# Expert 0's rows turned by one-hot products, gate and up weights in runs of 4 KB, rows of x taken with a step of two

## The chip, the core and the metric

The kernel runs on one core of a Trainium2 chip. The metric is the device time of one execution in microseconds. Five engines run their own instruction streams and meet at semaphores: TensorE (PE: products, with PEld for the loads of its fixed operand), VectorE (DVE), ScalarE (ACT), GpSimd (POOL) and SyncE (SP). SP's and GpSimd's streams also issue the DMA transfers.

## What is computed

One layer of a hybrid model on 512 tokens of width 1024, in f32: norm, input projection, sliding-window attention beside chunkwise retention, output projection with a residual, norm (its result is called h2), then a mixture of 16 gated experts, a residual and a last norm. The part that matters here is the mixture:

```python
p_group = softmax(hf @ rg_w + rg_b)             # 4 groups
g_prob, g_idx = top_k(p_group, 1)
e_logits = (hf @ re_w + re_b)                   # 4 experts in each group
...
top_p, top_i = top_k(softmax(sel), 2)           # two experts of that group
w = g_prob * top_p / sum(top_p)
...
for e in range(16):
    y = (silu(h @ w_gate[e]) * (h @ w_up[e])) @ w_down[e]
    out = out + combine[:, e:e + 1] * y
```

The kernel computes each expert only for the tokens that chose it.

## The kernel before, in words

**Products in two parts.** An f32 operand is split into a high part (a rounded copy, made by ScalarE) and a low part (the rest, made by VectorE), and a product is three products: high by high, high by low, low by high (`triple`, lines 1493 to 1497). So each weight passes through ScalarE (`split`, line 890) and VectorE (`split`, line 1302) before TensorE can use it.

**The dense part** (0 to 235 us) works through 15 groups of weights, `STEPS`; the last tiles of the output projection (`N1 - 2`, `N1 - 1`) interleave with the router's logits (line 1664), the second norm (`norm2`, line 1173) and the gate (`gate`, line 1198).

**The expert part.** An expert's weights are six chunks of 1 MB: two of gate, two of up, two of down. They are numbered n = 0, 1, ... in the order in which TensorE uses them: gate of expert 0 is 0 and 1, up 2 and 3, gate of expert 1 is 4 and 5, down of expert 0 is 6 and 7, and so on, six further for each expert. SP loads them into a ring of twelve raw slots (lines 461 to 486), ScalarE and VectorE split them into rings of three high and three low slots. A chunk is 12 products of 512 columns. So the split of chunk n waits for product n - 3.

The order within a step of expert e is written out by hand for each engine, with c = 0 to 5 for the chunks 6e + 4 + c:
- TensorE (`step`, line 1817): up product, transposes of `hid` and of the rows for expert e + 2 (`turn_rows`, line 1786), the gate product of e + 1 around them, the down product.
- ScalarE (`step`, line 902): six splits, the high part of the turned rows (`rows_hi`) and of the turned hidden tile, `silu`; and at the end the two halves of `y` (line 929), which scale the result by the token's weight in `row_info` and so wait for `info_ready`.
- VectorE (`step`, line 1382): six splits, `hid` = silu times up, the low parts of the hidden tile (`row_lo`) and of the rows (`rows_lo`).
- GpSimd (`traffic`, line 616): gathers the rows for expert e + 4 (`gather`), then copies `row_info` (`info_ready`), then scatters `y`. `gather` and `send_rows` read an expert's length, in quarters of 128, from field 3 of `meta` (`by_length`, line 580).

**Between the two parts.** For each token VectorE finds its two experts (`gate`: `pair_hot`, `pair_any`) and its place in their lists (`find_ranks`, from products with a triangle of ones), then marks that place in a one-hot tile (`mark`, line 1237). TensorE multiplies these with token numbers (`list_fields`) and gets, for each expert, the list of its tokens; VectorE copies it to `meta` (line 1322, `lists_ready`). h2 itself has gone to DRAM by then (line 564), and GpSimd gathers from it the rows of experts 0 and 1 (line 575). TensorE turns them (line 1856 on), ScalarE and VectorE split them, and the first product starts. `keep_clock` (line 1505) issues 33 products whose result nobody reads. While the gather runs, VectorE computes the weights of the tokens (lines 1325 to 1350). After the first rows and split 2 it makes the slots for long lists (1357 to 1364) and the flags `over`, which tell whether a list is longer than 128 (1366 to 1379, `over_set`); ScalarE waits for `over_set` before its first `silu` (line 935), since `route`, which these instructions use, lies in the buffer of `y`. SP holds its loads from chunk 8 on until the rows of expert 0 have landed (line 470).

**Names in the diff.** `h2_buf`: two buffers for h2, used in turn, that become `x_rows`, the gathered rows. `route`: VectorE's working area. `y_buf`: the two buffers for `y`.

Of the kernel before, what the change touches and what calls it, by code (L numbers as in the profile page):

```python
# [134 lines left out]
def build(nc, x, norm1_g, w_in, attn_sinks, rel_bias, ret_gn_g, w_out, norm2_g, rg_w, rg_b, re_w, re_b,  # L135
          w_gate, w_up, w_down, final_g, table, out):
    ctx = ExitStack()
    with ctx:
# [11 lines left out]
        def dram(name, shape, dt):  # L150
# [23 lines left out]
        y_buf = [nc.alloc_sbuf_tensor_at("y0", [P, D], F32, offset=at_hi + 2560 * 4),  # L174
                 nc.alloc_sbuf_tensor_at("y1", [P, D], F32, offset=at_lo + 2560 * 4)]
# [42 lines left out]
        h2_buf = [region(O_XG, D), region(O_XG + D, D)]  # L218
# [3 lines left out]
        x_rows = h2_buf  # L222
# [27 lines left out]
        route = y_buf[0][:, 0:1024]  # L250
# [21 lines left out]
        w_gate_v = w_gate.rearrange("a e (k p) n -> (a e) p k n", p=P)  # L272
        w_up_v = w_up.rearrange("a e (k p) n -> (a e) p k n", p=P)
# [28 lines left out]
        h2_out = [h2_out, sem("h2_out1")]  # L302
# [4 lines left out]
        hot_ready, index_ready = sem("hot_ready"), sem("index_ready")  # L307
        weights_set, weights_made, info_made = (sem(n) for n in ("weights_set", "weights_made", "info_made"))
# [88 lines left out]
        def _(sp):  # L397
# [48 lines left out]
            def load_expert(kind, e, half, slot):  # L446
                w = {"g": w_gate_v, "u": w_up_v}
                if kind == "d":
                    sp.dma_start(as_chunks(raw(slot), 2 * SEG), w_down_v[e][:, 2 * half:2 * half + 2, :]).then_inc(w2_in[slot], 16)
                else:  # L450
                    sp.dma_start(as_chunks(raw(slot)), w[kind][e][:, 4 * half:4 * half + 4, :]).then_inc(w2_in[slot], 16)
# [9 lines left out]
            for n in range(RING2):  # L461
# [8 lines left out]
                if n == RING2 - 4:  # L470
                    sp.wait_ge(rows_in[0], 16)
# [16 lines left out]
            def load_unit(r, e, c):  # L488
                for half in range(2):
                    for i, w in enumerate((w_gate_v, w_up_v)):  # L490
                        sp.dma_start(as_chunks(raw(2 * i + half)), w[bass.ds(e, 1), :, 4 * half:4 * half + 4, :]
                                     .rearrange("e p k n -> (e p) k n")).then_inc(ov_w, 16)
# [19 lines left out]
        def _(pool):  # L512
# [49 lines left out]
            for t in range(T - 1):  # L562
                pool.wait_ge(h2_ready, t + 1)
                pool.dma_start(h2_dram[t * P:(t + 1) * P, :], h2_buf[t % 2]).then_inc(h2_out[t % 2], 16)
            index_records(1, 0, EARLY)
            pool.wait_ge(h2_ready, T)
            pool.dma_start(h2_dram[(T - 1) * P:, :], h2_buf[(T - 1) % 2]).then_inc(h2_out[(T - 1) % 2], 16)
            index_records(2, EARLY, T)

            last_token, last_row = pool.to_reg(S - 1), pool.to_reg(2 * S - 1)  # L570
            for b in range(2):
                pool.wait_ge(h2_out[b], 16 * T // 2)
            pool.wait_ge(lists_ready, 1)
            for b in range(2):
                pool.indirect_dma_start(x_rows[b], None, h2_dram, bass.IndirectOffsetOnAxis(ap=meta[:, 4 * b:4 * b + 1], axis=0),
                                        bounds_check=last_token, oob_is_err=False).then_inc(rows_in[b], 16)
            pool.dma_start(gain2, bass.AP(final_g.tensor, 0, [[0, P], [1, D]])).then_inc(gain_in, 16)
            pool.wait_ge(info_made, 1)
# [16 lines left out]
            def gather(b, e):  # L595

                nc.gpsimd.tensor_copy(gather_idx[:, b:b + 1], meta[:, bass.ds(e * 4, 1)]).then_inc(idx_ready, 1)
                pool.wait_ge(idx_ready, e - 1)
# [17 lines left out]
            def traffic(b, e, gather_next, reuse, last=False):  # L616
                if gather_next:
                    pool.wait_ge(x_turned, e * 2 + 6)
                    pool.wait_ge(rows_in[b], e * 8 + (32 - 8 * b))
# [14 lines left out]
            gather(1, 3)  # L634
            for e in range(2):
# [51 lines left out]
        def _(act):  # L687
# [197 lines left out]
            act.wait_ge(gate_d, 1)  # L885
            nc.scalar.activation(route[:, 848:868], route[:, 848:868], ACT.Exp).then_inc(gate_e, 1)
            nc.scalar.activation(stat[:, 47:48], eps[:, 0:1], ACT.Silu)

# [7 lines left out]
            def rows_hi(b, wait):  # L896
                for a in range(2):
# [4 lines left out]
            def step(b, e, q, first=False, last_two=False):  # L902
# [30 lines left out]
            rows_hi(0, 1)  # L933
            split(3, 3, 16)
            act.wait_ge(over_set, 1)
# [12 lines left out]
            for i in range(2):  # L948
                act.wait_ge(info_ready, E - 1 + i)
                if i:  # L950
                    act.wait_ge(y_sent[0], 16 * (E // 2 - 1))
# [33 lines left out]
        def _(dve):  # L985
# [187 lines left out]
            def norm2(t):  # L1173
# [3 lines left out]
                if t >= 2:  # L1177
                    dve.wait_ge(h2_out[t % 2], 16)
                nc.vector.scalar_tensor_tensor(h2_buf[t % 2], res_t[:, t, :], rms[:, T + t:T + t + 1], gain2,
# [18 lines left out]
            def gate(t0, t1):  # L1198
# [23 lines left out]
                nc.vector.tensor_scalar(pair_any[:, t0 * E:t1 * E], flat, 2.0, None, ALU.is_lt).then_inc(pair_ready, 1)  # L1222
                pairs = [P, 2, (t1 - t0) * E]
# [4 lines left out]
            def find_ranks(t0, t1, ahead):  # L1228
# [6 lines left out]
                step_done(nc.vector.tensor_reduce(rank_tiles[:, :, t0:t1], picked_tiles[:, :, t0:t1, :], AX_X, ALU.add))  # L1235

# [72 lines left out]
            def rows_lo(b, wait):  # L1309
                for a in range(2):  # L1310
                    row_lo(xt[b][1][:, 4 * a:4 * a + 4, :], 4 + a, xt[b][0][:, 4 * a:4 * a + 4, :], x_hi, wait + a, x_lo)

            find_ranks(0, EARLY, ps[:, 1, 0:EARLY * E])
            mark(0)
            norm2(T - 1)
            gate(EARLY, T)
            mark(1)
            find_ranks(EARLY, T, ps[:, 2, 0:(T - EARLY) * E])
            for t in range(EARLY, T):
                mark(t)  # L1320
            dve.wait_ge(lists_made, 1)
# [3 lines left out]
            step_done(nc.vector.tensor_reduce(g_top, lg[:, :, 0, :], AX_X, ALU.max))  # L1325
            nc.vector.tensor_tensor(g_exp, lg[:, :, 0, :], g_top.unsqueeze(2).to_broadcast([P, T, 4]), ALU.subtract)
# [653 lines left out]
```

## Time and profile before

| what | value |
|---|---|
| median of 3 runs (lowest, highest) | 552.3 us (551.95, 555.5) |
| profiled execution: own time, span | 552.4 us, 550.6 us |
| PE, DVE, ACT, POOL busy in the span | 98%, 77%, 64%, 17% |
| chain that ended last, by engine | PE 88%, DVE 5%, ACT 2%, DMA 2%, issue 1% |
| last tile of the output projection added to the residual (VectorE) | 235.45 |
| lists copied to `meta` (`lists_ready`) | 242.95 to 243.14 |
| first gather issued | 244.03 |
| rows of expert 0 turned from | 248.97 |
| product 0, product 4, product 5 start | 251.04, 264.24, 268.27 |
| SP issues chunk 8 | 248.95 |

Times in the lower half are microseconds from the start of the span. A matmul is shown from its start to its modelled end, and the next starts before that end, so the length of a chunk is read from start to start. "Idle" on an engine counts only where the engine is what the end waits for.

### The profile page before, as it was taken

What the parts mean: (1) busy time and instruction counts of PE and PEld (TensorE: products, weight loads), DVE (VectorE), ACT (ScalarE), POOL (GpSimd) and SP (SyncE); (2) the same over time, 40 slices, a digit from 0 to 9 for tenths busy, and PEclk for the clock granted to TensorE, in tenths of its full rate; (3) what the DMA queues carried; (4) which work ended last, traced back from release to release, by engine and by line L of the source; (5) the groups of instructions that cost most, each with busy time, mean ns of one, the idle gap of its engine ahead of it and who ended that gap; (6) DMA issues with size and microseconds to landing.
All of it is one profiled execution on the core that took longest, in us unless ns stands there. A gap on an engine that the chain in (4) does not pass through costs nothing.

```text
span 550.6 us, 7873 instructions
## 1 busy us (share of the span) xinstructions
PE 536.9 (98%) x2662; PEld 438.5 (80%) x2663; DVE 421.3 (77%) x580; ACT 353.3 (64%) x470; POOL 91.3 (17%) x113
## 2 busy tenths in 40 slices
PE   7999999999999999999999999999999999999995
PEld 5988777777877888877788888888888888888883
DVE  5654599554864753588989898988989898988986
ACT  5563654780326253355778978788778978788745
POOL 3260000000000000031412222022212222110420
PEclk9999999999999999999999999999999999999998
DMA  8999122323020237639999999999999999999796
GB/s 322 371 283 401 42 71 77 76 79 77 0 77 0 78 114 251 234 138 313 349 380 373 379 394 382 367 371 376 392 352 374 375 390 373 376 390 393 251 208 212
DMA packets 63821, 144.03 MB, mean 262 GB/s; under 512 B 3833, under 2 KB 13361, under 8 KB 63665
## 3 DMA queue, kind: packets, MB, share of 16 engines
q1 hardware_dynamic: 56528, 120.24, 61.4%
q0 software_dynamic: 7120, 22.90, 13.7%
q10 hardware_dynamic: 144, 0.52, 0.3%
q8 instruction: 15, 0.25, 0.2%
q14 instruction: 14, 0.11, 0.1%
HBM read 132.77 MB, written 14.30 MB: 267 GB/s over the span
## 4 chain that ended last, share of the span: by engine, by line
PE 88%; DVE 5%; ACT 2%; DMA 2%; issue 1%; POOL 0%; DVEq 0%; POOLq 0%
PE ps L1495 25%; PE ps L1497 24%; PE ps L1496 24%; PE ps L1502 7%; PE ps L1646 2%; PE ps L1632 2%; PE ps L1608 1%; PE ps L1578 1%; PE ps L1673 1%; DMA arena<-h_dram,meta 1%; DMA arena<-norm_g 1%; DVE lo_ring L1305 1%; DVE act_lo L1015 1%; PE ps L1896 1%; DVE res L1474 0%
## 5 line engine op out<-in xcount | busy, mean ns | idle before, releaser
L1305 DVE TENSOR_TENSOR lo_ring<-arena,hi_ring 128x2048 fp32r<-128x2048 f32 x94 | 213.8, 2288 | 26.9 <-ACT hi_ring L894 26.8
L1495 PE MATMUL ps<-hi_ring,act_hi 128*128 128x512 f32 x576 | 229.8, 399 | 1.5 <-DVE lo_ring L1305 1.1
L1497 PE MATMUL ps<-hi_ring,act_lo 128*128 128x512 f32 x576 | 224.9, 390 | 0.0
L1496 PE MATMUL ps<-lo_ring,act_hi 128*128 128x512 f32 x576 | 224.4, 390 | 0.0
L894 ACT ACTIVATE hi_ring<-arena 128x2048 fp32r<-128x2048 f32 x94 | 180.2, 1917 | 28.1 <-PE ps L1497 28.1
L1495 PEld LDWEIGHTS ps<-hi_ring,act_hi 128*128 128x128 f32 x576 | 108.3, 188 | 23.5 <-issue 2.4
L1497 PEld LDWEIGHTS ps<-hi_ring,act_lo 128*128 128x128 f32 x576 | 108.1, 188 | 23.3
L1496 PEld LDWEIGHTS ps<-lo_ring,act_hi 128*128 128x128 f32 x576 | 108.4, 188 | 20.9
L1005 DVE SCALAR_TENSOR_TENSOR lo_ring<-arena,over,hi_ring 128x512 fp32r<-128x512 f32 x40 | 29.2, 747 | 29.4 <-ACT hi_ring L708 29.2
L1015 DVE TENSOR_TENSOR act_lo<-ps,act_hi 128x512 fp32r<-128x512 f32 x56 | 36.7, 683 | 7.6 <-ACT act_hi L742 5.6
L600 POOL DMA_INDIRECT arena<-h_dram,gather_idx x14 | 34.7, 2478 | 24.0 <-issue 24.0
L1502 PE MATMUL ps<-keep,arena 128*128 128x128 f32 x268 | 36.9, 279 | 1.6 <-DMA arena<-h_dram,meta 1.2
L1502 PEld LDWEIGHTS ps<-keep,arena 128*128 128x128 f32 x268 | 30.7, 143 | 6.6 <-issue 1.9
L606 POOL DMA_INDIRECT y_dram<-y,row_info x14 | 13.2, 943 | 98.5 <-issue 98.5
L708 ACT ACTIVATE hi_ring<-arena,over 128x512 fp32r<-128x512 f32 x40 | 27.5, 718 | 0.4 <-DVE over L1035 0.4
L554 POOL DMA_DIRECT2D arena<-norm_g x1 | 0.6, 556 | 153.4 <-PE ps L1502 153.4
L1495 PE MATMUL ps<-act_hi,hi_ring 128*128 128x256 f32 (+1 forms) x64 | 22.0, 343 | 0.5 <-DVE act_lo L1015 0.5
L914 ACT ACTIVATE act_hi<-ps 128x512 fp32r<-128x512 f32 x15 | 9.0, 599 | 19.8 <-PE ps L1502 19.8
L1496 PE MATMUL ps<-act_lo,hi_ring 128*128 128x256 f32 (+1 forms) x64 | 21.5, 336 | 0.0
L1497 PE MATMUL ps<-act_hi,lo_ring 128*128 128x256 f32 (+1 forms) x64 | 21.5, 336 | 0.0
L929 ACT ACTIVATE y<-ps,row_info 128x512 f32<-128x512 f32 x28 | 19.0, 680 | 3.1 <-PE ps L1497 3.1
L1294 DVE TENSOR_TENSOR res<-res,ps 128x512 f32<-128x512 f32 x8 | 5.5, 687 | 18.6 <-PE ps L1497 18.6
(237 smaller groups left out, 523.0 us busy)
## 6 DMA issues: line engine op xcount, KB each, us to landing
arena<-w_gate SPq DMA_DIRECT2D x32, 1024.0 KB, 16.6
arena<-w_up SPq DMA_DIRECT2D x32, 1024.0 KB, 17.6
arena<-w_down SPq DMA_DIRECT2D x32, 1024.0 KB, 15.2
arena<-w_in SPq DMA_DIRECT2D x16, 512.0 KB, 7.2
y_dram<-arena POOLq DMA_DIRECT2D x8, 512.0 KB, 11.2
res<-y_dram POOLq DMA_DIRECT2D x8, 512.0 KB, 9.8
arena<-w_in SPq DMA_DIRECT2D x2, 1024.0 KB, 10.9
arena<-w_out SPq DMA_DIRECT2D x4, 512.0 KB, 6.5
```

The costliest lines, as they stand in the source:

```text
L600: by_length(e, lambda n: pool.indirect_dma_start(x_rows[b][0:n, :], None, h2_dram, bass.IndirectOffsetOnAxis(ap=gather_idx[0:n, b:b + 1], ...
L606: by_length(e, lambda n: pool.indirect_dma_start(y_dram, bass.IndirectOffsetOnAxis(ap=row_info[0:n, 4 * b + 1:4 * b + 2], axis=0), y[0:n, ...
L708: ins = nc.scalar.activation(dst, src, ACT.Copy, scale=gain)
L894: nc.scalar.activation(hi(N1 + n12), raw(n12), ACT.Copy).then_inc(hi_done, 1)
L929: nc.scalar.activation(y_buf[b][:, a * 512:(a + 1) * 512], ps[:, 2 + a, :], ACT.Copy, scale=row_info[:, 4 * b + 2:4 * b + 3].bitcast(F32)) ...
L1005: ins = nc.vector.scalar_tensor_tensor(dst, src, gain, src_hi.bitcast(F32), ALU.mult, ALU.subtract)
L1015: nc.vector.tensor_tensor(dst, ps[:, bank, :].rearrange("p (k s) -> p k s", k=4), src_hi.bitcast(F32), ALU.subtract).then_inc(done, 1)
L1305: nc.vector.tensor_tensor(lo(N1 + n12), raw(n12), hi(N1 + n12).bitcast(F32), ALU.subtract).then_inc(lo_done, 1)
L1495: nc.tensor.matmul(dst, a_hi, b_hi, start=start, stop=False)
L1496: nc.tensor.matmul(dst, a_hi, b_lo, start=False, stop=False)
L1497: return nc.tensor.matmul(dst, a_lo, b_hi, start=False, stop=stop)
L1502: ins = nc.tensor.transpose(ps[:, bank, i * P:(i + 1) * P], blk, ident)
```

## The change

**The rows of expert 0.** VectorE's new `find_first` makes, for each of the four token tiles, a one-hot tile of the token's place in the list of expert 0 (`first_hot`). TensorE multiplies h2, still in SBUF, with it (`first_rows`: four f32 products for each tile and half), and the sum over the four tiles is the block of expert 0's rows, already turned. For that, h2 stays in four places (`h2_home`), two of them in raw slots 9 and 10. The gather of expert 0 goes; GpSimd gathers experts 1 and 2 instead, after `lists_ready` and `x_turned` 2, and the loop's gathers begin with expert 3. The filler products go.

**What is reordered.** All `mark`s come after the last ranks. The list products come after the one-hot products, and VectorE reads the lists after the first half of the rows, two split pieces and the second half. The weights' list products come after products 0 and 1. GpSimd computes part of the gate (`diff`, `g_exp`, its sums). ScalarE does split 2 first, loads the tables early, and does the exponential between the two halves of the rows. `set_lengths` (field 3 of `meta`) moves into VectorE's step of expert 0 behind `row_lo` of the hidden tile, and GpSimd waits for it (`lengths_made`) before its gather of expert 3. `set_slots` moves to c = 4 of expert 0, the flags and sums of `over` to c = 0, 2 and 5 of expert 1; ScalarE waits for `over_set` before `y` of expert 1 and not before the first `silu`. SP's loads wait for the last store of h2 (chunk 8) and for `x_turned` (chunks 9 and 10).

**Weights and columns.** Gate and up chunks are read so that a partition gets two neighbouring rows of the weight (4 KB in a run). To match, the turned blocks hold every second column of x: `row_cols`, used by `first_rows`, `turn_rows` and the long-list path.

The diff, cut to its core:

```diff
+        h2_home = [region(O_BIAS, D), region(O_BIAS + D, D), x_rows[1], x_rows[0]]
+        first_hot = region(O_BIAS + 2 * D, T * P).rearrange("p (t s) -> p t s", t=T)
...
-        w_gate_v = w_gate.rearrange("a e (k p) n -> (a e) p k n", p=P)
+        w_gate_v = w_gate.rearrange("a e (h g p j) n -> (a e) p h g (j n)", h=2, g=2, p=P)
...
@@ SP
-                if n == RING2 - 4:
-                    sp.wait_ge(rows_in[0], 16)
+                if n == O_BIAS // GRAN - 1:
+                    sp.wait_ge(h2_out[T - 1], 16)
+                elif n == O_BIAS // GRAN:
+                    sp.wait_ge(x_turned, 1)
+                elif n == O_BIAS // GRAN + 1:
+                    sp.wait_ge(x_turned, 2)
...
@@ GpSimd
             pool.wait_ge(lists_ready, 1)
-            for b in range(2):
-                pool.indirect_dma_start(x_rows[b], ...
+            pool.wait_ge(x_turned, 2)
+            for e in (1, 2):
+                pool.indirect_dma_start(x_rows[e % 2], ...
             pool.dma_start(gain2, ...
-            pool.wait_ge(info_made, 1)
+            pool.wait_ge(lengths_made, 1)
...
-            pool.wait_ge(x_turned, 2)
-            pool.wait_ge(rows_in[0], 16)
-            gather(0, 2)
             pool.wait_ge(y_zeroed, 16 * 2 * T)
             pool.wait_ge(x_turned, 4)
             pool.wait_ge(rows_in[1], 16)
             gather(1, 3)
+            pool.wait_ge(info_made, 1)
             for e in range(2):
                 traffic(e, e, True, False)
...
@@ ScalarE
                 if not first:
                     act.wait_ge(y_sent[b], e * 8 - 8 * b)
+                elif b:
+                    act.wait_ge(over_set, 1)
                 act.wait_ge(info_ready, e + 1)
...
-            act.wait_ge(over_set, 1)
             act.wait_ge(mm_done, used_value(N1 + 1))
...
@@ VectorE
+            def find_first(t0, t1, ahead):
+                last = t1 == T
+                step_done(nc.vector.tensor_scalar(miss[:, t0:t1], standing[:, t0:t1, 0, 0], 2.0, 2.0 * S, ALU.is_ge, ALU.mult))
+                dve.wait_ge(rank_ready, 2 if last else 1)
+                step_done(nc.vector.tensor_tensor(first_rank[:, t0:t1], ahead, miss[:, t0:t1], ALU.add))
+                for t in range(t0, t1):
+                    nc.vector.tensor_scalar(first_hot[:, t, :], order, first_rank[:, t:t + 1], None,
+                                            ALU.is_equal).then_inc(first_hot_set, 1)
...
+            def step(b, e, last=False, first=False):
                 for c in range(PER_E):
                     split(e * PER_E + 4 + c, (4 + PER_E * b + c) % RING2)
+                    if first and c == 0 and b == 0:
+                        rows_lo(1, 3)
+                    if first and c == 0 and b:
+                        set_flags()
+                    if first and c == 2 and b:
+                        sum_flags((1, 2, 4))
+                    if first and c == 4 and b == 0:
+                        set_slots()
+                    if first and c == 5 and b:
+                        sum_flags((8, 16, 32))
+                        nc.vector.tensor_copy(over[:, UNITS + 1:2 * UNITS + 1], flags[0]).then_inc(over_set, 1)
...
                     if c == 2:
                         row_lo(hid_t[1], 6, hid_t[0], hid_hi, e + 1, hid_lo)
+                        if first and b == 0:
+                            set_lengths()
...
@@ TensorE
+            def row_cols(a, i):
+                c0 = 4 * a * P + i // 2 * 2 * P + i % 2
+                return slice(c0, c0 + 2 * P - 1, 2)
+
+            def first_rows(t, a):
+                pe.wait_ge(h2_ready, t + 1)
+                pe.wait_ge(first_hot_set, t + 1)
+                for i in range(4):
+                    ins = nc.tensor.matmul(ps[:, 4 + a, i * P:(i + 1) * P], h2_home[t][:, row_cols(a, i)],
+                                           first_hot[:, t, :], start=(t == 0 and i == 0), stop=(t == T - 1 and i == 3),
+                                           skip_group_check=True)
+                return ins
+
+            first_rows(0, 0)
             logits(2 * T - 1)
-            keep_clock(2, 0)
+            first_rows(0, 1)
+            first_rows(1, 0)
...
             ins.then_inc(rank_ready, 1)
-            pe.wait_ge(onehot_ready, EARLY)
-            list_fields(7, 0, 1, False, False)
-            keep_clock(1, 0)
+            first_rows(1, 1)
+            for a in range(2):
+                first_rows(2, a)
+                first_rows(3, a).then_inc(x_turned, 1)
...
-                    turn(4 + a, [x_rows[b][:, (4 * a + i) * P:(4 * a + i + 1) * P] for i in range(4)]
+                    turn(4 + a, [x_rows[b][:, row_cols(a, i)] for i in range(4)]
...
+            pe.wait_ge(x_lo, 1)
+            product(0, xt[0], 0, 0, 0, True, False)
+            pe.wait_ge(x_lo, 2)
+            product(0, xt[0], 4, 1, 1, False, True)
             pe.wait_ge(weights_set, 2)
```

## Rows read from the trace of the kernel before

**Rows 1.** Stages: length, busy us of PE, PEld, DVE, ACT, POOL, clock, DMA share, GB/s.

```profile
237.00:248.00 11.00, 10.31 (x52) 7.66 (x51) 9.75 (x36) 5.49 (x7) 4.90 (x6) 1.00 0.22 79
248.00:258.00 10.00, 8.85 (x47) 7.56 (x48) 8.35 (x33) 3.40 (x4) 1.23 (x2) 1.00 0.88 295
286.00:540.00 254.00, 254.00 (x1197) 211.69 (x1196) 226.85 (x155) 205.29 (x171) 57.89 (x58) 1.00 1.03 361
```

**Rows 2.** The chain that ended last: start us, length us, engine, line.

```profile
132.31 2.23 PE ps L1646 x20
...
267.21 1.31 PE ps L1502 x12
...
284.88 1.31 PE ps L1502 x12
```

**Rows 3.** The page, DMA issues: count, KB each, us to landing.

```profile
arena<-w_gate SPq DMA_DIRECT2D x32, 1024.0 KB, 16.6
...
arena<-w_down SPq DMA_DIRECT2D x32, 1024.0 KB, 15.2
```

**Rows 4.** Timeline of VectorE: start us, length us, then the instruction.

```profile
240.64 0.18 DVE L1222 TENSOR_SCALAR y<-y 128x32 bf16<-128x32 f32 x1
...
254.79 0.32 DVE L1368 TENSOR_SCALAR y<-y 128x16 f32<-128x16 f32 x3
...
256.30 0.24 DVE L1376 COPY y<-y 128x8 f32<-128x8 f32 x1
...
257.38 0.19 DVE L1379 CAST over<-y 128x48 int32<-128x48 f32 x1
...
269.01 0.68 DVE L1015 TENSOR_TENSOR act_lo<-ps,act_hi 128x512 fp32r<-128x512 f32 x1
...
279.27 4.50 DVE L1305 TENSOR_TENSOR lo_ring<-arena,hi_ring 128x2048 fp32r<-128x2048 f32 x2 [0.94 <-ACT hi_ring L894]
...
293.73 2.29 DVE L1305 TENSOR_TENSOR lo_ring<-arena,hi_ring 128x2048 fp32r<-128x2048 f32 x1 [0.26 <-ACT hi_ring L894]
```

**Rows 5.** Timeline of TensorE, in brackets its idle time before.

```profile
249.82 1.04 PE L1760 MATMUL ps<-act_lo 128*128 128x32 f32 x8
...
264.24 0.47 PE L1495 MATMUL ps<-hi_ring,act_hi 128*128 128x512 f32 x1 [1.13 <-DVE lo_ring L1305]
...
281.99 0.39 PE L1495 MATMUL ps<-hi_ring,act_hi 128*128 128x512 f32 x1
```

**Rows 6.** Line 575, the first two gathers.

```profile
DMA to landing us min/median/max: 4.9/5.6/6.4
```

**Rows 7.** Line 600, the loop's 14 gathers.

```profile
DMA to landing us min/median/max: 8.1/8.7/9.8
```

**Rows 8.** Timeline of GpSimd.

```profile
260.51 0.18 POOL L597 COPY gather_idx<-meta 128x1 int32<-128x1 int32 x1 [3.14 <-issue]
262.33 2.60 POOL L600 DMA_INDIRECT arena<-h_dram,gather_idx  x1 [1.64 <-issue]
268.59 0.55 POOL L597 COPY gather_idx<-meta 128x1 int32<-128x1 int32 x1 [3.65 <-PE ps L1502]
270.72 2.55 POOL L600 DMA_INDIRECT arena<-h_dram,gather_idx  x1 [1.58 <-issue]
273.27 0.20 POOL L623 COPY row_info<-meta 128x3 int32<-128x3 int32 x1
```

**Rows 9.** Timeline of ScalarE.

```profile
275.91 0.67 ACT L929 ACTIVATE y<-ps,row_info 128x512 f32<-128x512 f32 x1
276.75 0.69 ACT L929 ACTIVATE y<-ps,row_info 128x512 f32<-128x512 f32 x1 [0.16 <-PE ps L1497]
277.33 1.91 ACT L894 ACTIVATE hi_ring<-arena 128x2048 fp32r<-128x2048 f32 x1
```

**Rows 10.** Stages at the end, columns as in rows 1.

```profile
545.00:546.00 1.00, 0.00 (x0) 0.00 (x0) 1.00 (x1) 0.96 (x3) 0.00 (x0) 1.00 0.59 242
547.00:548.00 1.00, 0.00 (x0) 0.00 (x0) 0.58 (x1) 0.00 (x0) 0.00 (x0) 0.50 0.96 389
```

More of the change, by code:

```diff
@@ L894, in split, with rows_hi @@
                 nc.scalar.activation(hi(N1 + n12), raw(n12), ACT.Copy).then_inc(hi_done, 1)
-            def rows_hi(b, wait):
-                for a in range(2):
+            def rows_hi(b, wait, halves=range(2)):
+                for a in halves:
                     act.wait_ge(x_turned, wait + a)
@@ L950, in _ @@
                 if i:
[L951 removed]
+                    act.wait_ge(y_sent[1], 16 * (E // 2 - 1))
                 for a in range(2):
@@ L1379, in _, with set_lengths @@
-            nc.vector.tensor_copy(over[:, UNITS + 1:2 * UNITS + 1], flags[cur]).then_inc(over_set, 1)
-            def step(b, e, last=False):
+            def set_lengths():
+                step_done(nc.vector.tensor_scalar(quarters, count, float(QUARTER), None, ALU.is_gt))
+                for i in (2, 3):
+                    step_done(nc.vector.scalar_tensor_tensor(quarters, count, float(QUARTER * i), quarters,
+                                                             ALU.is_gt, ALU.add))
+                nc.vector.tensor_copy(meta_v[:, :, 3:4], quarters.unsqueeze(2)).then_inc(lengths_made, 1)
@@ new lines, in _, with set_flags, sum_flags @@
+            flags = [r(64 * i, UNITS) for i in range(2)]
+            def set_flags():
+                for i in range(1, S // P):
+                    ins = nc.vector.tensor_scalar(flags[0][:, (i - 1) * E:i * E], count, float(P * i), None, ALU.is_gt)
+                step_done(ins)
+                nc.vector.tensor_copy(over[:, 0:UNITS], flags[0])
+                step_done(nc.vector.memset(over[:, UNITS:UNITS + 1], 0))
+            def sum_flags(shifts):
+                for shift in shifts:
+                    cur = (shift.bit_length() - 1) % 2
+                    a, b = flags[cur], flags[1 - cur]
+                    nc.vector.tensor_copy(b[:, 0:shift], a[:, 0:shift])
+                    step_done(nc.vector.tensor_tensor(b[:, shift:], a[:, shift:], a[:, 0:UNITS - shift], ALU.add))
@@ L1390, in step @@
                         row_lo(hid_t[1], 6, hid_t[0], hid_hi, e + 1, hid_lo)
+                        if first and b == 0:
+                            set_lengths()
                     if c == 3 and not last:
                         rows_lo(b, e * 2 + 5)
-            split(3, 3)
-            rows_lo(1, 3)
-            with dve.Fori(0, E // 2 - 1) as q:
+            for e in range(2):
+                step(e, e, first=True)
+            with dve.Fori(1, E // 2 - 1) as q:
                 for b in range(2):
@@ L1876, in multiply_unit @@
                 for a in range(2):
-                    ins = turn(4 + a, [x_rows[0][:, (4 * a + i) * P:(4 * a + i + 1) * P] for i in range(4)])
+                    ins = turn(4 + a, [x_rows[0][:, row_cols(a, i)] for i in range(4)])
                 ins.then_inc(ov_pe, 1)
```

150 lines of the change are left out of this document (69 added, 81 removed).

## The prediction

> **What bounds the kernel now.** I read the stages first (the table of windows), then the chain that ended last, then the timelines of the four engines from 228 to 310 us. In the expert loop, 286 to 540 us, TensorE is busy in all 254.00 us and the other engines are not [rows 1]: an expert takes 17.67 us of products and transposes (284.88 - 267.21 [rows 2]), and nothing but TensorE's own work counts there. A transfer is worth nothing in that stretch unless it comes late. The stretch that the change is about is the one before it, 237 to 264 us, where the chain leaves TensorE: gate, ranks, lists, the gather of expert 0's rows, their transposes, the two halves of their split, and VectorE's bookkeeping. TensorE looks busy there only because of the filler products of `keep_clock`. DMA is nearly idle, a share of 0.22 in 237 to 248, since the weight loads wait for that gather [rows 1].
>
> All times below are on the clock of the profiled execution: its span is 550.6 us and its own time 552.4, so 1.8 us lie around the span. The median of the runs is 552.3, so the sum is made against 552.4.
>
> **Weights in runs of 4 KB.** Same bytes, same number of transfers, half the runs. `w_down` has 4 KB runs already and lands in 15.2 us, `w_gate` in 16.6 [rows 3]. So a load lands between 0 and about 1.4 us sooner. TensorE has no idle time in the loop for a load to fill, so I take 0: what hides it is the ring of twelve slots, two experts deep. If loads came late instead, that cover would be gone and the loop would stretch; with fewer runs for the same bytes I see no reason for it.
>
> **Rows taken with a step of two.** Each expert has 8 transposes whose loaded operand now has a step of two floats. In the trace every operand that is loaded lies side by side, so none shows the cost. The bounds are 0 (the load reads as fast) and a load twice as long: 0.109 us more for each transpose (12 of them take 1.31 us [rows 2]), 8 for each of 15 experts, 13.1 us, all on the path. I take 0, and keep 13.1 as a rival.
>
> The Trainium skill, "Advanced Engine Details and Errata", section "SBUF Cachelines", says that a read wants at least two hits in a line of 16 bytes and is slower when each access opens a new line. A step of two floats is 8 bytes, which is just two hits, so by that rule the price is 0; no run here shows it yet, and it is why I give the rival little.
>
> **One-hot products in place of list and gather.** These are plain f32 products, and the trace records two passes for each: 20 passes of 128 columns at line 1646, which computes 10 products, take 2.23 us, 0.112 each [rows 2]. One call of `first_rows` is 4 products, 8 passes, 0.9 us; there are 8 calls, 7.2 us. They replace 33 filler products, so TensorE has the room. Up to the second ranks little moves: VectorE's new `find_first` costs some 0.2 us against the `mark` that it pushes back, so `pair_ready`, 240.82 before [rows 4], comes at 241.0 and the ranks end at 241.3. Three calls are done by then; the other five end at 245.8, the list products (8 in 1.04 us [rows 5]) at 246.7. ScalarE and VectorE split the first half in that time (0.68 us on VectorE [rows 4], about the same on ScalarE). Product 0 starts at 246.7, product 1 ends at 252.2, the weights' list products at 253.2, product 2 at 255.9 (2.73 us for 12 passes).
>
> Next comes a transposition of expert 1's rows, and here the gather returns. The lists are now read late: VectorE has rows and two split pieces ahead of them, so `lists_ready` comes at 247.4, and GpSimd issues 0.9 us behind it, as in the table above, at 248.3. The same gather landed in 4.9 to 6.4 us when the weight loads waited for the first of them [rows 6]; now they don't, and under weight loads a gather takes 8.1 to 9.8 [rows 7]. I take 8.1, since this form issues faster: 256.4. Turned at 257.4, product 3 ends at 260.2, and product 4 starts there. Before it starts at 264.24 [rows 5]. **The lead is 4.1 us** (4.6 if the gather is early, 2.4 if it lands in 9.8).
>
> **First wait that moves: the lengths.** `set_lengths` was done before the loop. Now it stands in VectorE's step of expert 0, behind `row_lo` of the hidden tile, which ended at 269.69 [rows 4] and now ends at 265.6; with some 0.85 us for its four small instructions, each waiting for the one before (an estimate by the flags, three in 0.32 without such waits), `lengths_made` comes at 266.4. GpSimd waits for it before `gather(1, 3)`, and behind that stand `gather(0, 4)` and the copy of `row_info` that sets `info_ready`. Before, the first of these gathers was done at 264.9, while TensorE was still at expert 0. From the rows: 1.82 + 2.60 for the first, 2.13 + 2.55 for the second, 0.20 for the copy, 9.3 us, so `info_ready` at 275.8 [rows 8]. ScalarE needs it for `y` of expert 0, at 275.91 before [rows 9], but now at 271.8. It stands there for 4 us, and the next weight split is queued behind it: 0.58 us a half, 1.91 the split [rows 9], 2.3 the low half, product 10 at about 281.5. Before it starts at 281.99 [rows 5]; without the wait it would be 277.9. **3.6 us of the lead go.**
>
> **Second wait: the flags.** The 18 small instructions that end with `over_set` took 254.79 to 257.57 ahead of the loop [rows 4], with ScalarE waiting. Now they are in VectorE's step of expert 1: the flags (three in 0.32 us, some 0.55 with a cast and a memset) sit ahead of split 11 and of `hid`, and TensorE waits some 0.6 us for `hid`. The last three sums and the copy (256.30 to 257.57, 1.27 us) come after VectorE's split 15, which ends at 296.02 in the old schedule, and ScalarE waits for `over_set` before `y` of expert 1, which it began one expert after 275.91, at 293.6. So `y` starts at 297.3, 3.7 late, and split 16 behind it. One expert earlier the low half of split 10 ends at 281.56 [rows 4] for a product that starts at 281.99, so that chain has 0.4 us to spare. **0.6 + 3.3 us are lost.** After that every step has its old order and nothing is late, but nothing is caught up either, as TensorE has no idle time in the loop.
>
> The sum: -4.1 + 3.6 + 0.6 + 3.3 = +3.4, 552.4 + 3.4 = **555.8 us**. GpSimd's own arithmetic (7 small instructions for the gate; an estimate of 0.2 to 0.35 us each by the 0.20 of its copy [rows 8]) ends near 244.6, a microsecond before the second half of the rows; at twice that it is still hidden, behind VectorE's split pieces. Bounds below the sum: both waits hide after all, and the hidden tile's too, 548.3. Above it: the latest gather, 557.5.
>
> **Rivals.**
> *The waits cost nothing* (faster side): ScalarE reaches `y` after `info_ready` and `over_set`, or GpSimd's two gathers are quicker than 2.6 us each. Then the lead of 4.1 to 4.6 stays: 548 us. It decides at `y` of expert 0: if it starts before 273, this is the case. Against it stands the program order, which has both waits ahead of a weight split. If only one of the two is hidden, 552. Chance 0.22 for both.
> *TensorE's clock falls in the two new gaps*: each is about 3.2 us, and the longest that the rows show is 1.13 [rows 5]. At the end, with TensorE idle, the granted clock was 1.00 in 545 to 546 and 0.50 in 547 to 548 [rows 10]: it fell from 2.4 to 1.2 GHz after TensorE's work had ended. If it falls in a gap, the product behind it takes up to 2.73 us more: 556 to 561, about 559. Chance 0.12. The Trainium skill, "TensorE: Matmul & The Clock Gate", section "HAM oscillation — how this bites in real kernels", says that waits between bursts of matmuls put the array back to half rate; by that rule this rival is the case, and the trace agrees only for the idle end.
> *The step of two is paid for*: 13.1 us for the transposes and up to 7 for the one-hot products, 569 to 576. Chance 0.07.
> The forecast itself has 0.59.
>
> **How the numbers follow.** 1% is 5.5 us, about what a measurement of this kernel can tell from no change. Forecast and half-hidden cases are within 1%, and of the first rival most (548 is 0.8% off; 0.05 beyond 546.9). Slower by over 1% (from 557.9): the stride, most of the clock case, the latest gathers: 0.17. Same: 0.78. The range leaves out the stride and the best of the first rival: 548.0 to 559.5; the forecast's own is 553.5 to 557.5.
>
> **What would show it.** Right: product 0 some 4 us earlier; `y` of expert 0 within 0.5 us of 275.9 and right behind `row_info`; an idle row of about 3 us in front of a product near 281 and of another near 302, released by VectorE's low half; 17.67 us an expert after that, at a clock of 1.00. Wrong: no such gaps (first rival), a granted clock below 1.00 near 282 or 303 (second), 12 transposes in 2.2 us in place of 1.31 (third), or a product 0 later than 249, which would mean that the one-hot products cost more than 0.9 us a call.

## Result: 562.6 us, slower, and outside the range

The changed kernel took 562.6 us, the median of four runs (561.5 to 564.8), against 552.2 before (552.3 in the table above, which has one run less): a ratio of 1.018, 95% interval 1.013 to 1.023. So it is slower; whether by more than 2% is open. The forecast was 555.8 with a range up to 559.5, so the sign was right and the size was not. The profiled execution took 561.5 us with a span of 559.9, 9.3 more than the span before, and these 9.3 are what is taken apart here.

Each expert's turn shows in the chain of waits as one row of 12 transposes, so its starts are a ruler. Where TensorE did not wait, the chain starts such a row some 0.2 us later than the timeline does, so a single stretch is good to about 0.2 us. The chain of the kernel after:

```profile
263.98 1.56 PE ps L1557 x12
...
279.64 0.68 ACT y L952
280.32 1.81 ACT hi_ring L915
282.15 2.30 DVE lo_ring L1344
284.58 0.77 PE ps L1550
...
288.88 1.39 PE ps L1557 x12
...
301.70 0.68 ACT y L952
...
306.56 0.50 PE ps L1550
...
311.00 1.59 PE ps L1557 x12
328.95 1.39 PE ps L1557 x12
```

And three rows of the chain of the kernel before that go on from [rows 2]:

```profile
302.56 1.31 PE ps L1502 x12
320.25 1.31 PE ps L1502 x12
...
497.11 1.31 PE ps L1502 x12
```

The row that answers to 497.11 starts at 506.28 in the kernel after. Stretch by stretch:

| stretch | before | after | difference |
|---|---|---|---|
| to the last tile of the output projection | 235.45 | 235.35 | -0.1 |
| from there to the 12 transposes of expert 0 | 31.76 | 28.63 | -3.1 |
| to those of expert 1 | 17.67 | 24.90 | +7.2 |
| to those of expert 2 | 17.68 | 22.12 | +4.4 |
| to those of expert 3 | 17.69 | 17.95 | +0.3 |
| ten more experts | 176.86 | 177.33 | +0.5 |
| the rest | 53.49 | 53.62 | +0.1 |

So the lead is there, and two experts give back almost four times as much (11.7 us against 3.1). Both times the chain leaves TensorE in the same order: `y`, the high split queued behind it, the low split, the product. TensorE's timeline after, with the idle time in brackets, shows the two gaps and a smaller one ahead of product 0 (line 1832 is the list products, 261.10 the start of product 4, 310.80 the transposes behind the second gap):

```profile
245.75 1.04 PE L1832 MATMUL ps<-act_lo 128*128 128x32 f32 x8
248.20 0.47 PE L1550 MATMUL ps<-hi_ring,act_hi 128*128 128x512 f32 x1 [1.40 <-DVE lo_ring L1027]
...
261.10 0.39 PE L1550 MATMUL ps<-hi_ring,act_hi 128*128 128x512 f32 x1
...
284.58 0.77 PE L1550 MATMUL ps<-hi_ring,act_hi 128*128 128x512 f32 x1 [5.34 <-DVE lo_ring L1344]
...
306.56 0.50 PE L1550 MATMUL ps<-hi_ring,act_hi 128*128 128x512 f32 x1 [2.67 <-DVE lo_ring L1344]
...
310.80 0.84 PE L1557 MATMUL ps<-keep,hid 128*128 128x128 f32 x4
```

What `y` waited for stands in ScalarE's timeline, `row_info` the first time and the flags the second:

```profile
279.05 1.26 ACT L952 ACTIVATE y<-ps,row_info 128x512 f32<-128x512 f32 x2 [6.03 <-POOL row_info L650]
...
301.11 1.26 ACT L952 ACTIVATE y<-ps,row_info 128x512 f32<-128x512 f32 x2 [3.36 <-DVE over L1437]
```

Behind both gaps products run slower, 0.43 us apart in place of 0.23: behind the first at once, behind the second from 307.84 on, 1.3 us after they had begun again. The stages of the kernel after, columns as in [rows 1]:

```profile
284.00:287.00 3.00, 2.42 (x6) 1.96 (x7) 2.93 (x7) 1.71 (x1) 0.00 (x0) 0.50 0.78 265
...
308.00:311.00 3.00, 3.00 (x9) 2.22 (x8) 3.00 (x3) 0.00 (x0) 0.00 (x0) 0.50 0.89 355
320.00:540.00 220.00, 220.00 (x1040) 184.10 (x1038) 196.81 (x123) 179.80 (x148) 49.70 (x51) 1.00 0.95 345
```

A granted clock of 0.50 is 1.2 GHz in place of 2.4. The last row answers to the third of [rows 1]: TensorE is again busy throughout at 1.00, and the DMA engines are busy 0.95 of the time where 1.03 stood.

Why the first gap is 5.3 us and not 3.6 is to be seen on GpSimd (answers to [rows 8]):

```profile
267.47 2.16 POOL L624 COPY gather_idx<-meta 128x1 int32<-128x1 int32 x1 [15.84 <-DVE meta L1395]
271.56 2.34 POOL L627 DMA_INDIRECT arena<-h_dram,gather_idx  x1 [1.93 <-issue]
273.91 2.31 POOL L624 COPY gather_idx<-meta 128x1 int32<-128x1 int32 x1
277.82 1.00 POOL L627 DMA_INDIRECT arena<-h_dram,gather_idx  x1 [1.60 <-issue]
278.83 0.19 POOL L650 COPY row_info<-meta 128x3 int32<-128x3 int32 x1
```

and on VectorE at the same time:

```profile
267.22 0.18 DVE L1395 CAST meta<-y 128x16 int32<-128x16 f32 x1
267.30 2.29 DVE L1344 TENSOR_TENSOR lo_ring<-arena,hi_ring 128x2048 fp32r<-128x2048 f32 x1
...
273.90 2.28 DVE L1344 TENSOR_TENSOR lo_ring<-arena,hi_ring 128x2048 fp32r<-128x2048 f32 x1
```

Two copies of one column, 0.18 and 0.55 us in [rows 8], take 2.16 and 2.31, and each ends within 0.05 us of the end of a split on VectorE (269.59 and 276.18).

### The profile page after: what moved, and what is told of

It reads as the page before. It is cut to its first block, busy times and chain, and to the rows that moved or that the text cites. A ratio compares the mean times of both kernels' runs of the same rounds, so it can differ in the third digit from the quotient of the medians.

```text
span 559.9 us, 7913 instructions
## 1 busy us (share of the span) xinstructions
PE 539.6 (96%) x2685; PEld 442.6 (79%) x2686; DVE 422.0 (75%) x584; ACT 352.9 (63%) x471; POOL 92.0 (16%) x118
## 4 chain that ended last, share of the span: by engine, by line
PE 89%; DVE 5%; ACT 3%; issue 1%; DMA 1%; POOL 0%; ACTq 0%; DVEq 0%; POOLq 0%
PE ps L1550 25%; PE ps L1552 24%; PE ps L1551 24%; PE ps L1557 7%; PE ps L1701 2%; PE ps L1687 2%; DVE lo_ring L1344 1%; PE ps L1663 1%; PE ps L1728 1%; PE ps L1633 1%; ACT hi_ring L915 1%; DMA arena<-norm_g 1%; PE ps L1820 1%; PE ps L1960 1%; DVE res L1529 0%
## 5 line engine op out<-in xcount | busy, mean ns | idle before, releaser
L1557 PEld LDWEIGHTS ps<-keep,arena 128*128 128x128 f32 x260 | 31.9, 173 | 4.9 <-issue 1.9
L627 POOL DMA_INDIRECT arena<-h_dram,gather_idx x13 | 30.5, 2350 | 22.7 <-issue 22.7
L633 POOL DMA_INDIRECT y_dram<-y,row_info x14 | 13.1, 937 | 99.7 <-issue 99.7
L624 POOL COPY gather_idx<-meta 128x1 int32 (+1 forms) x13 | 6.5, 503 | 89.3 <-PE ps L1557 73.5
```

Of the source, the lines that this page charges most:

```text
L627: by_length(e, lambda n: pool.indirect_dma_start(x_rows[b][0:n, :], None, h2_dram, bass.IndirectOffsetOnAxis(ap=gather_idx[0:n, b:b + 1], ...
L633: by_length(e, lambda n: pool.indirect_dma_start(y_dram, bass.IndirectOffsetOnAxis(ap=row_info[0:n, 4 * b + 1:4 * b + 2], axis=0), y[0:n, ...
L1557: ins = nc.tensor.transpose(ps[:, bank, i * P:(i + 1) * P], blk, ident)
```

## Experiments

The theory: the two waits and what hangs on them (copies held by splits, the clock behind the gaps) make the loss, and the part that shortens the front works. The rivals: the way in which the loop reads its data costs the time; GpSimd is slow by itself; VectorE has no room for what was moved into the loop. Each ratio below is to the kernel before, run again beside its set (552.5 us for the first four kernels, 553.0 for the next four, 552.1 for the last three); a difference of medians between sets is good to about a microsecond. Four kernels ran first.

**Lengths ahead of the loop.** `set_lengths` goes back to where the kernel before had it; all else as changed.

```diff
+            set_lengths()
...
                     if c == 2:
                         row_lo(hid_t[1], 6, hid_t[0], hid_hi, e + 1, hid_lo)
-                        if first and b == 0:
-                            set_lengths()
```

> The changed kernel took 562.6 us; its trace has TensorE idle for 5.3 us ahead of product 10, and about 3 us of products at half rate behind that, which cost 1.6 us more. Theory (the wait for lengths_made): with the lengths made ahead of the loop, info_ready comes before ScalarE reaches y of expert 0, the gap and the half rate behind it go, and 562.6 - 6.9 = 555.7 us are left; the gap of 2.7 us ahead of product 16 stays, since over_set still stands behind VectorE's split of chunk 15. Rival 1 (GpSimd is slow by itself: its copies of an index column took 2.16 and 2.31 us where 0.2 is usual, and its two gathers 2.3 and 1.0 us): info_ready still comes 2 us or more after ScalarE's split, and the time is 559 to 560. Rival 2 (the loss is in how the loop reads its data, and the gap only shows it): 562 or more.

Measured: 555.1 us, median of ten (ratio 1.0052, 1.0027 to 1.0076). The first gap is gone, the second is there:

```profile
300.04 0.50 PE L1550 MATMUL ps<-hi_ring,act_hi 128*128 128x512 f32 x1 [2.73 <-DVE lo_ring L1344]
```

The theory holds: the wait for four small instructions, with the held copies and the half rate that hung on it, cost 7.5 us. The rival of the slow GpSimd fails here, since its copy of the same kind, at 259.18 in this kernel, took 0.18 us beside a subtraction of VectorE that reads one operand from PSUM (258.73 to 260.02).

**Flags in a buffer of their own.** The sums stay in the step of expert 1, but ScalarE need not wait for them.

```diff
-            flags = [r(64 * i, UNITS) for i in range(2)]
+            flags = [rw[:, 64 * i:64 * i + UNITS] for i in range(2)]
...
-... r(868, 2 * T), r(876, E)
+... r(868, 2 * T), rw[:, 144:144 + E]
...
-                    act.wait_ge(over_set, 1)
+                    act.wait_ge(slots_ready, 1)
```

> The flags and their sums keep their place in VectorE's step of expert 1 but lie in another buffer than y of expert 1, so ScalarE's y waits for the slots only, which are made an expert earlier. Theory (the wait for over_set): the gap of 2.7 us ahead of product 16 and the half rate behind it (1.5 us) go, the first gap stays: 562.6 - 4.2 = 558.4 us. Rival (the wait is only the last of several that end together, such as row_info behind the late gather of expert 5): the gap stays within 1 us of 2.7 and the time is 561.5 to 562.6.

Measured: 557.8 us (1.0094, 1.0066 to 1.0122). The second gap is gone and the first is left (5.33 us), so the second wait, too, is what the chain says. The same sums on the same engine leave no gap there once nobody waits for their buffer.

**Both.**

> Lengths ahead of the loop and flags in their own buffer, both together. Theory: both gaps and both stretches at half rate go, 562.6 - 6.9 - 4.2 = 551.5 us, 0.8 below the kernel before: the lead of 3.2 us stands, less some 0.6 us for the step of two (17.73 us an expert where 17.69 were) and less what VectorE's added instructions cost in experts 0 and 1. Rival (VectorE has only about 1.5 us to spare in an expert, and the 18 instructions of the flags and the 5 of the slots take 3.8 us over two experts): new gaps of 1 to 2 us ahead of products 11 to 18, 553 to 554 us.

Measured: 551.1 us, median of ten (0.9979, 0.9953 to 1.0006): neither gap is left, and the kernel is no longer slower than before. The chain of this kernel shows what remains in the first experts:

```profile
264.59 1.56 PE ps L1557 x12
...
281.91 0.69 DVE hid L1443
282.64 1.62 PE ps L1557 x12
300.62 1.39 PE ps L1557 x12
318.37 1.39 PE ps L1557 x12
```

18.05 and 17.98 us for two stretches, 17.75 for the third. `hid` of expert 1 is late: on VectorE it stands behind the flags, and the transposes start as it ends. That of expert 2 is in time (ready at 300.24, the transposes start at 300.46); the rest of the second stretch is the restart behind the wait and the ruler's 0.2 us. By the timeline the two stretches together take 0.45 us more than two later ones. That is the rival of the full VectorE, at 0.45 us and not at 1 to 2.

**Columns and long runs alone,** on the kernel before (gate and up weights in 4 KB runs, `row_cols` in its three places).

> The kernel before with nothing but the gate and up weights in runs of 4 KB and the step of two in the rows of x; list and gather, waits and filler products as before. Theory: 0.04 to 0.05 us for each of some 15 experts, 552.3 + 0.7 = 553.0 us, and weight loads that land in about 7 us where 16.6 were, which no engine waits for. Rival 1 (the step of two is paid as a load twice as long): 565 us. Rival 2 (the loads in longer runs free something that TensorE waits for): 551 us or less.

Measured: 554.3 us, ratio 1.0018 (1.0002 to 1.0034), some 1.0 us more than before by the ratio. An expert takes 17.73 us here too, and 12 transposes 1.39. The second half of the expectation missed: loads land in 17.2 to 18.1 us, not in 7.

Then four that price single steps.

**Product 0 waits for its own pieces only,** on top of both.

```diff
-                pe.wait_ge(lo_done, n + (split_value(N1 + n12 + RING2) - n12 - RING2))
+                pe.wait_ge(lo_done, pieces or n + (split_value(N1 + n12 + RING2) - n12 - RING2))
...
-            product(0, xt[0], 0, 0, 0, True, False)
+            product(0, xt[0], 0, 0, 0, True, False, split_value(N1))
```

> On top of the kernel with early lengths and flags apart (551.1 us). Product 0 there waits until VectorE has written seven pieces of low halves, its own four and three of chunk 1, and TensorE stands 1.4 us for the third of them (idle row of 1.40 us ahead of the product at 248.78). Here it waits for its own four only. Theory (this wait is where 0.9 to 1.4 us of the forecast lead went): product 0 follows the list products without the idle time, and 549.7 us are left if nothing else is late; if the gather of expert 1's rows (8.6 to 9.8 us to landing) is late next, 0.4 to 0.9 us are left of that and the time is 550.2 to 550.7. Rival (product 0 is held by the second half of the rows or by the memory it shares with the split, not by this wait): 551.1, no change.

Measured: 550.3 us (0.9956, 0.9937 to 0.9975). TensorE's timeline:

```profile
245.74 1.04 PE L1832 MATMUL ps<-act_lo 128*128 128x32 f32 x8
246.64 0.48 PE L1550 MATMUL ps<-hi_ring,act_hi 128*128 128x512 f32 x1
...
256.51 1.23 PE L1557 MATMUL ps<-keep,arena 128*128 128x128 f32 x8 [0.50 <-DMA arena<-h_dram,meta]
```

Product 0 starts right behind the list products, and 0.5 us come back as a wait for the gather of expert 1's rows.

**Columns side by side, runs of 2 KB,** on top of both (the weights' views and `row_cols` as before the change).

> On top of the kernel with early lengths and flags apart (551.1 us): gate and up weights back in runs of 2 KB and the rows of x taken side by side. Theory (the step of two costs some 5 ns for each of 8 transposes of an expert, and the long runs give TensorE nothing): an expert takes 17.69 us again in place of 17.73, 550.4 us; loads land in 15 to 17 us in place of 7. Rival (the long runs keep some wait away, or the loads in short runs collide with the gathers at the start): 551.1 or more.

Measured: 549.3 us (0.9943, 0.9926 to 0.9960); an expert takes 17.67 us. That is 1.8 less than with both edits and 1.1 less than the theory said. The shorter expert explains 0.9 of it, 0.06 for each of 15; no run places the rest, and the runs with both edits spread from 550.1 to 555.3.

**Fillers in the first gap,** on the kernel with flags apart.

```diff
+                if b and isinstance(e, int):
+                    for _ in range(22):
+                        nc.tensor.matmul(ps[:, 7, :].rearrange("p (k s) -> p k s", k=4), upper_b,
+                                         ones_b.unsqueeze(1).to_broadcast([P, 4, P]), start=True, stop=True)
                 pe.wait_ge(x_lo, e * 2 + 4)
```

> On top of the kernel with the flags apart alone (557.8 us; first gap of 5.3 us, an expert of 25.41 us around it): 22 filler products of 512 columns, some 5.0 us, stand in TensorE's order ahead of product 10, so that it still starts when its low half is there, but TensorE has not been idle before it. Theory (the granted clock falls because of the idle time): clock 1.00 in 284 to 292, the products behind the gap 0.23 us apart, the expert 23.1 to 23.8 us long, 555.5 to 556.2 us. Rival (the products behind the gap are slow for another reason, such as the transfers or the split that run beside them): they stay 0.43 us apart and the time stays 557.8 or goes up by the part of the fillers that comes too late.

Measured: 556.9 us (1.0087, 1.0064 to 1.0110), 0.9 less than without them; in the profiles an expert of 23.91 us in place of 25.41. Timeline of TensorE, then the stage behind the gap:

```profile
278.57 4.92 PE L1898 MATMUL ps<-count_w 128*128 128x512 bf16 x22
284.07 0.47 PE L1550 MATMUL ps<-hi_ring,act_hi 128*128 128x512 f32 x1 [0.57 <-DVE lo_ring L1344]
...
287.37 0.66 PE L1557 MATMUL ps<-keep,hid 128*128 128x128 f32 x4 [0.29 <-DVE hid L1441]
```

```profile
284.00:288.00 4.00, 3.64 (x18) 2.81 (x19) 3.93 (x8) 1.20 (x1) 0.00 (x0) 1.00 0.81 298
```

The clock stays at 1.00 beside the same split and the same transfers, so it is the idle time that lets it fall. The time is 0.7 above the upper end of what was expected; part of that is `hid`, late next by 0.29 us, which half rate had hidden.

**No copies.** The changed kernel, where the gathers of experts 3 and 4 read their indices from `meta` itself.

```diff
-                nc.gpsimd.tensor_copy(gather_idx[:, b:b + 1], meta[:, bass.ds(e * 4, 1)]).then_inc(idx_ready, 1)
+                pool.sem_inc(idx_ready, 1)
...
-... bass.IndirectOffsetOnAxis(ap=gather_idx[0:n, b:b + 1], axis=0),
+... bass.IndirectOffsetOnAxis(ap=meta[0:n, 4 * e:4 * e + 1], axis=0),
```

> The changed kernel (562.6 us), with lengths and flags late as they are, but the gathers of experts 3 and 4 take their indices from the lists themselves, so GpSimd's two copies of an index column (2.16 and 2.31 us, each ending with the split that VectorE runs beside it) are gone. Theory (a GpSimd copy stands while VectorE's subtraction runs): the copies' 4 us go from the chain lengths_made to info_ready, but the copy of row_info that is left would then meet the split of chunk 9 and end with it near 276.2; y of expert 0 starts there in place of 279.05, the first gap shrinks from 5.3 to some 2.5 us, 559.8 us; if it meets no split, y starts near 274.7, 557 to 558 us. Rival (GpSimd takes that time for each gather anyway, in its descriptors, and the copies only show it): info_ready stays within 0.7 us of 279.0 and the time near 562.

Measured: 556.1 us (1.0074, 1.0051 to 1.0098). GpSimd:

```profile
269.71 1.04 POOL L636 DMA_INDIRECT arena<-h_dram,meta  x1 [17.84 <-issue]
271.42 2.67 POOL L636 DMA_INDIRECT arena<-h_dram,meta  x1 [0.67 <-issue]
274.09 0.20 POOL L659 COPY row_info<-meta 128x3 int32<-128x3 int32 x1
```

`row_info` starts 4.7 us sooner (274.09, 278.83 in the changed kernel) and takes 0.20; the first gap shrinks to 0.34 us and no half rate follows it. That is 6.5 us, more than either expectation: the copy of `row_info` met no split, and with a gap that short the clock stayed up. The first of these was luck: VectorE's next split began at 274.16, 0.07 us behind the copy. Two copies of 128 numbers stood for most of the first gap.

The last three put the parts together.

**Plain columns and product 0,** on top of both.

> Early lengths, flags apart, columns side by side with runs of 2 KB, and product 0 waiting for its own pieces only: all that the runs so far showed to pay. Theory (the parts add up): 549.3 (with plain columns) less some 0.8 (the wait of product 0, less 0.5 us of waiting for the gather) = 548.5 us, 3.8 to 4.2 below the kernel before. Rival (the gain of product 0 goes to the gather of expert 1's rows, which comes under loads in short runs, 8.1 to 9.8 us): 549.0 to 549.4.

Measured: 548.2 us (0.9931, 0.9918 to 0.9945). The parts add up. No version here took less; it is 3.8 us below the kernel before.

**Long runs, plain columns.** The one on top of both, with `row_cols` side by side and weights in 4 KB runs; the matching of the columns of x to the rows of the weights is left out.

> The kernel with early lengths and flags apart (551.1 us), weights in runs of 4 KB as there, but the rows of x taken side by side: the columns no longer match the rows of the weights, a part of the computation that is changed here and that no time depends on. Theory (the step of two is what an expert pays for): an expert takes 17.67 us, 12 transposes 1.31 us, about 550.2 us. Rival (the longer runs, whose transfers come in 7 us and in bursts, cost TensorE's reads the difference): an expert stays at 17.73 us and 12 transposes at 1.39, 551.1 us.

Measured: 549.1 us (0.9947, 0.9932 to 0.9961). Its chain:

```profile
299.47 1.32 PE ps L1557 x12
317.16 1.31 PE ps L1557 x12
334.82 1.31 PE ps L1557 x12
```

17.67 us an expert (17.69 and 17.66 here): the step of two is the cost. The runs are worth nothing that shows, 549.1 against 549.3, though loads land in 14.5 to 15.7 us in place of 15.6 to 17.0.

**Flags spread.** `set_flags` in VectorE's idle time ahead of split 5, sums (1, 2), (4, 8) and (16, 32) in steps of experts 0 and 1.

> On top of the kernel before it in this set, the flags are made in VectorE's idle microsecond ahead of split 5, and their sums two at a time in the steps of experts 0 and 1. Theory (in experts 1 and 2 the transposes wait some 0.3 us each for hid, because VectorE's added instructions stand ahead of it): both experts take 17.67 us, and 0.4 to 0.6 us are won, 548.0 us. Rival (VectorE has no time to spare in experts 0 to 2 wherever the instructions stand): the same time within 0.2 us.

Measured: 548.4 us (0.9940, 0.9925 to 0.9954), the same as without it, where the six runs of either kernel spread over 2.6 to 2.9 us. The chain:

```profile
262.29 1.53 PE ps L1556 x12
280.26 1.31 PE ps L1556 x12
297.95 1.31 PE ps L1556 x12
```

In this trace `hid` of expert 1 is no longer late (ready at 279.68, transposes at 280.10). That of expert 0 is (262.24, 262.29), as it was in the kernel before it (263.00, 263.06), where no flag stood ahead of it. By the timelines the two stretches take 35.50 us in place of 35.74. So the trace shows 0.24 of the 0.4 to 0.6 that the theory wanted, and the times can't tell that from the rival's nothing: this stays open.

## Why the prediction was wrong, step by step

Two steps failed above all. The 9.3 us from `lengths_made` to `info_ready` was too small, since two copies in it were held. And the sum put the clock behind the gaps that it forecast itself at nothing, where it cost 2.6 us.

**The lead: forecast 4.1, measured 3.1 at product 4** (261.1 against 264.24 in [rows 5]). The one-hot products cost what the row at line 1646 said, and the list products ended at 246.8, as forecast for product 0. But product 0 started at 248.20: its wait counts seven pieces of low halves, three of them chunk 1's. That formula stood in the kernel before, hidden by the late rows. I read the products' data and not their semaphore values. That is 1.5 us late; 0.5 of it the forecast had spent on waiting for the gather of expert 1's rows, which now came in time, so the lead is 1.0 short.

**The first wait: forecast a loss of 3.6, measured 5.3 idle plus the clock.** Place, order and mechanism were as written: lengths, two gathers, `row_info`, `y`, the split behind it. The term that failed is the 9.3 us from `lengths_made` to `info_ready`, which took 11.6 (267.40 to 279.02). I took 1.82 and 2.13 from [rows 8] for copy and issue; they took 4.09 and 3.91, while the two gathers took 1.8 us less than 2.60 and 2.55 (what makes such a gather take 1.0 or 3.0 us on GpSimd stays open). The copy of 0.55 us in [rows 8], three times its sister, was the hint: it ended at 269.14, as a split of VectorE did (269.09), and I read it as scatter. One expert on, the same trace has a second:

```profile
284.29 2.29 DVE L1305 TENSOR_TENSOR lo_ring<-arena,hi_ring 128x2048 fp32r<-128x2048 f32 x1
...
286.25 0.37 POOL L597 COPY gather_idx<-meta 128x1 int32<-128x1 int32 x1 [6.23 <-PE ps L1502]
```

The split ends at 286.58 and the copy at 286.62, and late in the loop copies of `row_info` take up to 1.65 us. A copy that starts when `lengths_made` is set starts just as VectorE goes on to its next split.

The experiment without copies shows their price. That VectorE's split holds them no experiment isolates, but all the profiles agree: between 236 and 548 us of the thirteen kernels 82 of GpSimd's 377 copies take over 0.25 us, and each of the 82 ends 0.03 to 0.06 us behind the end of a split. None that began inside a split with 0.2 us or more of it to run ended ahead of it. Beside a subtraction with an operand in PSUM a copy took 0.18 us.

The Trainium skill, "SBUF — State Buffer", section "Who interferes with whom", says it: a VectorE instruction with two SBUF inputs contends with a GpSimd instruction that reads SBUF. The trace agrees, 2.16 and 2.31 us for 0.18; I had not weighed that rule.

**The second wait: forecast 0.6 + 3.3, measured a gap of 2.7.** The mechanism is right. The late `hid` of expert 1 did not show behind the long first gap, and shows as 0.45 us once the gap is gone.

**The clock: a rival with 0.12, and it came true beside the forecast.** From the first of the products behind the first gap to the seventh it takes 2.70 us, and 1.46 in the kernel with fillers; behind the second gap twelve take 4.24 us to the transposes, 1.4 more than at full rate. Together that is some 2.6 us. I had split the chance between the gaps and the fallen clock as if one excluded the other. The fall needed only gaps of the size that I forecast myself, though not every such gap brings it (last section).

The Trainium skill, "TensorE: Matmul & The Clock Gate", section "HAM oscillation — how this bites in real kernels", which I named, says that such waits put the array back to half rate. The trace agrees behind both gaps of the changed kernel: clock 0.50, and 1.00 with fillers in the first.

**The step of two: bounds 0 and 13.1, taken 0.** It costs 0.04 to 0.06 us an expert (17.73 against 17.67 with both edits, against 17.69 on the kernel before), 0.6 to 0.9 in the loop. The lower bound was the nearer one, and too round.

By the rule of two hits in a line (the Trainium skill, "Advanced Engine Details and Errata", section "SBUF Cachelines") it would be 0; the measurement decides, and it is small and not 0.

**Long runs at 0: right.** From the forecast sum of 3.4 to the 9.3 of the profiles: lead +1.0, first wait +1.7, clock +2.6, step of two +0.7 (17.73 against the 17.69 before, and the transposes ahead of the loop), second wait -1.2. The other 1.1 is not placed singly: TensorE's restart behind each gap and four transposes at half rate are in it.

## What to carry to other kernels

Work that leaves the critical path must still be done before its reader asks: follow each moved instruction to the engine that waits for it, and to what is queued behind that engine; a free buffer removes such a wait without moving anything. Where a forecast has TensorE stand for microseconds, price the clock behind the gap as part of the same case. And a wait that is wider than its data, hidden today, is the next bound once the front gets shorter.

## What the runs showed that was not expected

- A gap of the same length does not always cost the clock. In the kernel with early lengths, 2.73 us ahead of product 16 left the granted clock at 1.00 in the profile, whose run took 553.4 us; the changed kernel's 2.67 us and 2.72 in the kernel without copies were followed by 0.50, in both about a microsecond after the products had begun again. Eight of the ten runs with early lengths took 554.5 us or more, so both may happen in one program; the cause stays open. The stage behind the gap with early lengths:

```profile
300.00:304.00 4.00, 3.96 (x22) 3.34 (x23) 4.00 (x3) 1.73 (x2) 0.00 (x0) 1.00 1.02 399
```

- The landing of 7 us in the changed kernel is no property of the long runs:

```profile
arena<-w_gate SPq DMA_DIRECT2D x32, 1024.0 KB, 6.9
...
arena<-w_down SPq DMA_DIRECT2D x32, 1024.0 KB, 7.5
```

  The same loads take 7 to 12 us where one gap is left, 14 to 16 where both are gone, and 17 to 18 in long runs on the kernel before. I take it that the loads caught up while the products stood still, and that each then found a shorter queue; no run here isolates that.

- Single runs of one kernel spread by up to 6.4 us (553.4 to 559.8 with early lengths). In the profile of the columns alone, 556.2 us, the granted clock over the first 120 us was 0.96, long before any changed line. So the small prices above are read from the length of an expert and not from single times.
